# At the two layer boundaries, GpSimd instead of VectorE multiplies x by the tile's rstd ahead of the transposes

## The reference

```
def rmsnorm(x, g):
    xf = x.astype(jnp.float32)
    y = xf * lax.rsqrt(jnp.mean(xf * xf, axis=-1, keepdims=True) + EPS)
    return (y * g.astype(jnp.float32)).astype(x.dtype)

def modulate(h, shift, scale):
    return h * (1 + scale[:, None, :]) + shift[:, None, :]
...
    for i in range(DEPTH):
        mod = jnp.einsum('bd,sdk->bsk', cond, ada_w[i]) + ada_b[i]
        ...
        h = modulate(rmsnorm(x, norm_g[i, 0]), shift_t, scale_t)
        if i % N_MIXERS == 0:
            y = pool_mixer(h, pool_w[i // N_MIXERS], pool_scale[i // N_MIXERS])
        else:
            y = retention(h, ret_w_in[i // N_MIXERS], ret_w_out[i // N_MIXERS])
        x = x + gate_t[:, None, :] * y
        h = modulate(rmsnorm(x, norm_g[i, 1]), shift_m, scale_m)
        x = x + gate_m[:, None, :] * sq_relu_mlp(h, mlp_w1[i], mlp_w2[i])
    return rmsnorm(x, final_g)
```

## Time and profile before

| what | us |
|---|---|
| median of 3 runs | 2530.89 (2526.59 to 2533.76) |
| the profiled execution | 2531.95 |
| its span, first to last instruction | 2530.1 |
| PE busy in the span | 2389.1 (94%) |
| DVE busy | 1570.2 (62%) |
| ACT busy | 1065.5 (42%) |
| POOL busy | 20.7 (1%), 30 instructions |

### The profile page before, as it was taken

One profiled execution on the slowest core, in us unless ns is written; L12 is line 12 of the kernel. 1 busy time (PEld: TensorE's weight loads), 2 busy tenths in 40 slices (PEclk: granted clock), 3 DMA queues, 4 the chain that ended last, 5 costly groups with the idle time before them and its releaser, 6 DMA issues.

```text
span 2530.1 us, 30014 instructions
## 1 busy us (share of the span) xinstructions
PE 2389.1 (94%) x10463; PEld 1862.7 (74%) x10463; DVE 1570.2 (62%) x1633; ACT 1065.5 (42%) x1315; POOL 20.7 (1%) x30
## 2 busy tenths in 40 slices
PE   4567699999999999999999999999999999999998
PEld 0023378888888888788888887888788888888886
DVE  3366577677677677775756666656777545445455
ACT  1022244344354444544445444444554453443443
POOL 0000000000000000000000000000000000000000
PEclk8578799999999999999999999999999999999999
DMA  8997888788788788577666776766698665656654
GB/s 307 319 322 266 299 302 300 242 299 291 247 303 294 262 298 283 192 254 227 218 218 230 232 233 216 233 216 224 232 329 276 178 190 189 187 187 195 186 181 158
DMA packets 269403, 620.89 MB, mean 245 GB/s; under 512 B 19064, under 2 KB 19400, under 8 KB 268360
## 3 DMA queue, kind: packets, MB, share of 16 engines
q1 hardware_dynamic: 268112, 612.65, 72.5%
q0 software_dynamic: 880, 5.77, 0.6%
q10 hardware_dynamic: 264, 0.52, 0.1%
HBM read 616.77 MB, written 2.10 MB: 245 GB/s over the span
## 4 chain that ended last, share of the span: by engine, by line
PE 89%; DMA 7%; DVE 2%; issue 1%; ACT 0%; SPq 0%; POOL 0%; ACTq 0%; POOLq 0%; DVEq 0%
PE acc L460 82%; DMA ada_raw<-in_ada_w 7%; PE tb L546 2%; PE mod_ps L571 1%; PE score_ps L571 1%; DVE w_lo L1151 0%; PE score_ps L762 0%; PE tb L649 0%; DVE h_lo L1317 0%; DVE ada_acc L1168 0%; PE acc L772 0%; PE acc L773 0%; PE acc L774 0%; DVE scratch L1305 0%; DMA raw<-in_mlp_w 0%
## 5 line engine op out<-in xcount | busy, mean ns | idle before, releaser
L1151 DVE TENSOR_TENSOR w_lo<-raw,w_hi 128x1024 fp32r<-128x1024 f32 x776 | 947.0, 1225 | 771.8 <-ACT w_hi L828 771.5
L828 ACT ACTIVATE w_hi<-raw 128x1024 fp32r<-128x1024 f32 x776 | 821.8, 1061 | 1155.5 <-PE acc L460 1068.7
L460 PE MATMUL acc<-w_hi,h_lo 128*128 128x512 f32 x1792 | 707.2, 395 | 9.7 <-DVE h_lo L1317 5.7
L460 PE MATMUL acc<-w_hi,h_hi 128*128 128x512 f32 x1792 | 699.0, 390 | 0.0
L460 PE MATMUL acc<-w_lo,h_hi 128*128 128x512 f32 x1792 | 698.6, 390 | 0.0
L460 PE MATMUL acc<-w_hi,a_lo 128*128 128x512 f32 x1312 | 517.9, 395 | 0.0
L460 PE MATMUL acc<-w_hi,a_hi 128*128 128x512 f32 x1312 | 511.9, 390 | 0.0
L460 PE MATMUL acc<-w_lo,a_hi 128*128 128x512 f32 x1312 | 511.8, 390 | 0.0
L1168 DVE SCALAR_TENSOR_TENSOR ada_acc<-ada_raw,cond,ada_acc 128x1024 f32<-128x1024 f32 x280 | 358.3, 1280 | 107.6 <-DMA ada_raw<-in_ada_w 107.2
L460 PEld LDWEIGHTS acc<-w_hi,h_lo 128*128 128x128 f32 x1792 | 337.4, 188 | 85.5 <-issue 8.9
L460 PEld LDWEIGHTS acc<-w_hi,h_hi 128*128 128x128 f32 x1792 | 337.1, 188 | 70.9
(11 more groups left out here) (122 smaller groups left out, 723.8 us busy)
## 6 DMA issues: line engine op xcount, KB each, us to landing
raw<-in_mlp_w SPq DMA_DIRECT2D x512, 512.0 KB, 4.6
ada_raw<-in_ada_w SPq DMA_DIRECT2D x384, 512.0 KB, 5.3
raw<-in_ret_w_in SPq DMA_DIRECT2D x192, 512.0 KB, 3.8
raw<-in_ret_w_out SPq DMA_DIRECT2D x64, 512.0 KB, 4.2
raw<-in_pool_w SPq DMA_DIRECT2D x8, 512.0 KB, 6.7
x<-in_x SPq DMA_DIRECT2D x2, 1024.0 KB, 11.7
scratch<-in_ada_b POOLq DMA_DIRECT2D x2, 1024.0 KB, 9.1
gate<-in_ada_b POOLq DMA_DIRECT2D x1, 1024.0 KB, 12.6
```

The lines of the kernel that those rows point to most:

```text
L460: mm = nc.tensor.matmul(acc[pair][t][:], l[:, CK * c + j, tok], w[:, c % RING, j, :], start=first and j == 0 and i == 0, stop=last and j = ...
L828: nc.scalar.activation(w_hi[:, c % RING], raw[:, c % RING], ACT.Copy).then_inc(hi_ready, 1)
L1151: nc.vector.tensor_tensor(w_lo[:, c % RING], raw[:, c % RING], w_hi[:, c % RING].bitcast(F32), ALU.subtract).then_inc(lo_ready, 1)
```

## The change

The eight multiplications of each boundary (two tiles, four blocks of 128 x 512) go from DVE's list to GpSimd's, right behind the power that makes their rstd. A `wait_ge` on rstd_done now orders GpSimd behind its own result. The last norm of the kernel, which scales its output on ACT and DVE, stays as it was (`tile_roots(False)`).

```
@@ VectorE @@
-            def scale_x(t):
-
-                dve.wait_ge(rstd_done, n.n["MS"])
-                for b in range(4):
-                    blk = slice(b * NB, (b + 1) * NB)
-                    nc.vector.tensor_scalar(x_scaled[:, t, blk], x[:, t, blk], rstd[:, t:t + 1], None,
-                                            ALU.mult).then_inc(xs_ready, 1)
...
                 lo(0)
-                scale_x(0)
                 gated(1)
...
                 split_part(0, 1, 1)
-                scale_x(1)
                 split_fill(0, 2)
@@ GpSimd @@
-            def tile_roots():
-                inverse_root(slice(0, 1))
-                inverse_root(slice(1, 2))
+            def scale_x(t):
+
+                pool.wait_ge(rstd_done, n.n["MS"])
+                for b in range(4):
+                    blk = slice(b * NB, (b + 1) * NB)
+                    nc.gpsimd.tensor_scalar(x_scaled[:, t, blk], x[:, t, blk], rstd[:, t:t + 1], None,
+                                            ALU.mult).then_inc(xs_ready, 1)
+
+            def tile_roots(scaled=True):
+                for t in range(TT):
+                    inverse_root(slice(t, t + 1))
+                    if scaled:
+                        scale_x(t)
...
-            tile_roots()
+            tile_roots(False)
```

## The result

| | us |
|---|---|
| before, median of 17 runs | 2530.89 (2526.59 to 2535.19) |
| changed kernel, median of 17 runs | 2537.38 (2532.95 to 2543.24) |
| ratio | 1.0026, 95% interval 1.0020 to 1.0033 |
| span of the profiled execution, before and after | 2530.1 and 2535.4 |

The change costs 6.5 us, 0.26%. Forecast were 2536 us, a range of 2532 to 2538.5, and "no change that shows", on the slow side. The number lies in that range; that it would not show is not borne out, since the interval of the ratio lies above 1. And the profile shows that the number came out right for reasons that are in good part others.

What follows compares the result with a forecast made beforehand. VectorE was taken to bound the boundaries, PE the stretch between. 16P - 7.0 with P = 0.75 gave +5.0 us on the median 2530.89: 2535.9, rounded to 2536, range 2532 to 2538.5.

Steps and rivals of the forecast that it cites:

- no change that shows: Whole kernel: the time moves by less than about 0.3% (7.6 us), on the slow side; chance of no change 0.70.
- its own signs: Wrong if a GpSimd block needs over 1.2 us, boundary PE idle differs over 5 us, or time moves elsewhere.
- What bounds a boundary of the kernel before, and that nothing is given back between them: VectorE bounds each boundary; between boundaries PE works 734.81 of 735.00 us, so boundary losses remain at the end.
- rival B: Both boundaries: no interference worth the name, PE starts earlier, -4.0 us in all (2527); chance 0.16.
- The price of one: P, one GpSimd multiplication of 512 columns at a boundary: 0.75 us, between 0.53 and 1.45.
- The two engines take turns at it, instruction by instruction: At boundaries, GpSimd's and VectorE's times add up beside weight splits, SBUF products or (less sure) casts; chance 0.46 with P 0.53 to 0.91.
- The sum 16P - 7.0: Both boundaries' net cost, 8P - 3.84 and 8P - 3.16: +5.0 us with P = 0.75.
- Its terms for tile 0: Tile 0's four GpSimd blocks less VectorE's saved scaling; at boundary 1 also less a 0.68 us addition: 4P - 1.58 - 0.68.
- Its terms for tile 1: Tile 1's four GpSimd blocks, all taking turns with VectorE, less its saved scaling: 4P - 1.58 at boundary 1.
- Rival A: Both boundaries: same turns but a dear GpSimd instruction, slower by over 7.6 us from P = 0.91; chance 0.26.
- The clock was 1.00 ... I count on the same: Both boundary windows: the clock stays at 1.00, as before with waits of up to 1.4 us.
- Edits at nothing: GpSimd's rstd wait, tile 1's power (late from P near 1.3), later DMAs and gate bias at boundaries: no cost.

Runs made afterwards that it cites:

- probe: A separate small kernel without the computation: GpSimd runs four instructions a phase, VectorE idle or running one kind; a 512-column multiplication alone took 1.55 us.

## Why the prediction was right, and where it was not

- **By its own signs**: the prediction called itself wrong if GpSimd needs over 1.2 us for one block, and it needs 1.55. That the time is as forecast is luck, as the sum below shows.
- **What bounds a boundary of the kernel before, and that nothing is given back between them**: right. The long window is as full as before, and without any scaling PE started tile 1 3.4 us earlier where rival B had 4.0. After the change it is GpSimd that PE waits for.
- **"The price of one", P = 0.75, bounds 0.53 and 1.45**: wrong, and outside both bounds: 1.55 alone, 1.56 to 2.71 in the kernel. The memset's pace of 0.86 ns a column was taken for that of arithmetic, which needs 2.5. The power of one column said nothing on it.
- **"The two engines take turns at it, instruction by instruction"**: right on GpSimd's side, wrong in size on VectorE's. GpSimd's first block did wait about as long as the weight split beside it still had to run. But a multiplication holds VectorE for 0.4 us of its 1.55 beside instructions with two SBUF inputs (0.7 beside casts). By the Trainium skill (SBUF — State Buffer, "Who interferes with whom") the one that comes second is blocked for the whole instruction of the other. The rows agree for GpSimd behind VectorE (1.55 becomes 2.9 beside subtractions of 1.16), and not for VectorE behind GpSimd.
- **The sum 16P - 7.0**: with the measured P it would give +17.8, and the measured cost is 6.5. Its terms for tile 0 were +0.74 and +1.42; PE starts tile 0 4.64 and 5.41 us later. Its terms for tile 1 were +1.42 each; from PE's start of tile 0 to that of tile 1 it takes 1.34 and 1.89 us less than before. By then VectorE is ahead, and PE waits 0.4 us for h_lo where it waited 2.9. So tile 0 was far too cheap in the sum and tile 1 too dear, and the two errors nearly cancelled: 3.30 and 3.52 us at the start of tile 1, 6.8 in all, where the sum had 5.0.
- **The wait of tile 0**: the prediction counted GpSimd's time as VectorE's, and had no term for PE waiting for tile 0's blocks. It is this that costs. In PE's list the transposes of all four blocks stand ahead of the first chunk, and the fourth block comes 7.2 us behind tile 1's last matmul. Rival A (a dear instruction) had the right cause, the wrong path, and a price of over 10 us.
- **"The clock was 1.00 ... I count on the same"**: wrong. Behind waits of 1 to 2 us in a row PE ran at the lower of its two levels (1.2 GHz), at boundary 1 until 1051.5, and the granted clock was 0.55 and 0.53 in a window of 6 us at each boundary. It costs 1.9 of the 6.97 us at boundary 1; its share at boundary 2 is open.
- **Edits at nothing**: right for the DMAs (the gate bias is issued at 1814.36, and nobody waits for it). The power of tile 1 was put at risk from P near 1.3; it did run late (1046.71, with the mean square there at 1046.39), with its cost covered by tile 0's delay.

## What to carry to other kernels

An engine with 1% of its time used is not a cheap place for work on a path: what counts is the length of one instruction there and who waits for it, and that length must be measured, not taken from another operation on the same engine. Ask for the idle stretch that lies at the right moment; here ScalarE had 2.14 us of it at boundary 1, just ahead of the need, and GpSimd's 99% was no help. And a forecast that comes true is no proof of its steps: here one probe showed two of them wrong.

## What the hardware showed that I had not expected

- GpSimd multiplies 128x512 float32 by a per-partition scalar in 1.55 us (by an immediate in 1.47), but a tensor of that size by itself, in the two-tensor form, in 1.01, and copies it in 0.57.
- One such instruction delays a queue of two-input VectorE instructions by 0.4 us, and the two-tensor form by 0.8 (17.09 us for twelve, 13.9 by proportion), while GpSimd itself is slowed by 1.0 to 1.4 us. Beside additions with one input in PSUM neither engine was slowed (6.19 us for GpSimd's four with and without them).
